# Inverse in tiles of 32 weight columns with its convolution taps moved, and the gate's input split during the PLE tiles

## The reference, cut to what matters

```python
qkv = silu(causal_conv(qkv, conv_buf, conv_w))          # four taps
a_mat = einsum("bnhid,bnhjd->bnhij", k_beta, k) * decay * strict
t_mat = triangular_solve(eye + a_mat, eye, lower=True, unit_diagonal=True)
...
e = rmsnorm(p_i @ w_proj, norm_w)                       # p_i has 256 columns
gate = sigmoid(h @ w_gate)                              # h has 2048 columns
h = h + e * gate
```

## Time and profile before

| | us |
| --- | --- |
| median of three runs | 2442.74 (2442.17 to 2444.59) |
| the profiled execution | 2443.26 |
| its span | 2441.5 |
| GDN loop, 15 passes | 971 |
| one pass of it | 63.54 |
| SSD loop and last body | 618 |
| first PLE step up to the second gate tile | 34 |
| PE busy | 2346.2 (96%) |
| POOL busy | 1762.6 (72%) |
| DVE busy | 1604.1 (66%) |
| ACT busy | 1260.5 (52%) |

### The profile page before, as it was taken

The page is one execution under the profiler, slowest core; times in us unless marked ns, Lnnn a source line. Parts: engine busy times, 40 slices in busy tenths (PEclk is TensorE's granted clock), DMA queues, the critical chain, the costliest instruction groups (busy, mean ns, idle before and its releaser), DMA issues.

```text
span 2441.5 us, 58796 instructions
## 1 busy us (share of the span) xinstructions
PE 2346.2 (96%) x21280; PEld 2201.1 (90%) x21280; DVE 1604.1 (66%) x3203; ACT 1260.5 (52%) x2201; POOL 1762.6 (72%) x2236
## 2 busy tenths in 40 slices
PE   5899999999999999999998989999999999999997
PEld 5799999999999999989998978989998999899897
DVE  7667666666666676661217466988898889712374
ACT  4555555555555555543335446555555555433443
POOL 5466566565555555558887968988898889789896
PEclk9999999999999999999999989999999999999998
DMA  5444444444444444436443445766576656554433
GB/s 200 149 156 148 155 155 148 151 142 148 144 155 147 148 143 143 146 114 222 155 164 134 163 152 204 239 202 202 189 240 212 198 193 229 189 182 155 155 136 123
DMA packets 126772, 410.84 MB, mean 168 GB/s; under 512 B 21344, under 2 KB 37984, under 8 KB 122112
## 3 DMA queue, kind: packets, MB, share of 16 engines
q1 hardware_dynamic: 80784, 294.49, 35.3%
q10 hardware_dynamic: 45936, 115.64, 14.0%
HBM read 363.47 MB, written 46.61 MB: 168 GB/s over the span
## 4 chain that ended last, share of the span: by engine, by line
PE 53%; POOL 32%; issue 10%; DVE 3%; ACT 1%; POOLq 0%; DMA 0%; DVEq 0%; ACTq 0%
POOL wl L335 32%; PE psj L358 14%; PE psj L359 12%; PE psj L360 12%; PE psA L393 2%; PE psC L393 2%; PE psE L393 2%; PE psD L504 1%; PE psA L569 1%; PE psC L519 1%; DVE xl L1398 1%; PE psA L382 1%; PE psE L535 0%; PE psE L387 0%; PE psC L387 0%
## 5 line engine op out<-in xcount | busy, mean ns | idle before, releaser
L335 POOL TENSOR_TENSOR wl<-ring,wh 128x256 fp32r<-128x256 f32 x2232 | 1762.4, 822 | 656.2 <-ACT wh L806 651.8
L358 PE MATMUL psj<-xh,wh 128*128 128x288 f32 x4400 | 1358.0, 309 | 37.2 <-DVE xl L1413 17.0
L359 PE MATMUL psj<-xl,wh 128*128 128x288 f32 x4400 | 1305.1, 297 | 0.0
L360 PE MATMUL psj<-xh,wl 128*128 128x288 f32 x4400 | 1300.3, 296 | 0.0
L358 PEld LDWEIGHTS psj<-xh,wh 128*128 128x128 f32 x4400 | 831.4, 189 | 90.9 <-issue 52.7
L806 ACT ACTIVATE wh<-ring 128x1024 fp32r<-128x1024 f32 x558 | 586.1, 1059 | 596.1 <-PE psj L360 556.9
L359 PEld LDWEIGHTS psj<-xl,wh 128*128 128x128 f32 x4400 | 834.2, 190 | 1.9
L360 PEld LDWEIGHTS psj<-xh,wl 128*128 128x128 f32 x4400 | 835.0, 190 | 0.0
L887 ACT ACTIVATE arena<-psj 128x256 f32<-128x256 f32 x112 | 42.8, 383 | 206.7 <-PE psj L360 200.5
L1768 DVE TENSOR_TENSOR h<-h,psj 128x288 f32 x32 | 14.5, 454 | 154.9 <-PE psj L360 154.9
L1839 DVE SCALAR_TENSOR_TENSOR arena<-arena 128x256 f32<-128x256 f32 x144 | 111.3, 799 | 3.4
(11 more groups left out here) (345 smaller groups left out, 2935.5 us busy)
## 6 DMA issues: line engine op xcount, KB each, us to landing
ring<-weights_d SPq DMA_DIRECT2D x558, 512.0 KB, 3.3
h<-gstate_d ACTq DMA_DIRECT2D x16, 1024.0 KB, 6.3
gst_s_d<-h ACTq DMA_DIRECT2D x16, 1024.0 KB, 3.9
h<-sstate_d ACTq DMA_DIRECT2D x32, 512.0 KB, 5.6
sst_s_d<-h ACTq DMA_DIRECT2D x32, 512.0 KB, 4.1
arena<-g_rows_d ACTq DMA_DIRECT2D x16, 864.0 KB, 6.0
arena<-s_rows_d ACTq DMA_DIRECT2D x8, 1152.0 KB, 8.7
h_spill_d<-h ACTq DMA_DIRECT2D x2, 2304.0 KB, 7.2
```

Source lines behind the costliest of these rows:

```text
L335: ins = pool.tensor_tensor(wl[:, s, n:n + 2], ring[:, s, n:n + 2], wh[:, s, n:n + 2].bitcast(F32), ALU.subtract)
L358: pe.matmul(out, w_h, xh[:, kt, :], start=(kt == 0), stop=False)
L359: pe.matmul(out, w_h, xl[:, kt, :], start=False, stop=False)
L360: mm = pe.matmul(out, w_l, xh[:, kt, :], start=False, stop=(kt == KT - 1))
```

## The change

Four parts. In `blocks` a call takes 32 weight columns instead of 64, so a group has twice the calls. The products read the same 32 columns of the right side as before. Of DVE's taps, the three prompt taps of v head 0 move from the inverse to the end of the pass before (`v_first`), between the norm and `Y`, with a wait for `took_act`. One tap of head 1 moves to the start of the body; the rest is spread anew, and the mask of level 4 comes behind the last sample taps. In the SSD loop two state products come one step later (46 and 56), and the sum one step later (71). In `ple` ACT and DVE split `h` during the projection, in slots 0 to 13 of `xh` and `xl`, while `dp` uses slots 14 and 15; the squares come later; and `e_sum` moves from step 4 to step 6.

```diff
-                for r in (0, 64):
-                    mm = pe.matmul(bank[r:r + 64, u * 32:(u + 1) * 32], lhsT[:, r:r + 64], rhs[:, in_block(r, lv), :],
+                for r in (0, 32, 64, 96):
+                    mm = pe.matmul(bank[r:r + 32, u * 32:(u + 1) * 32], lhsT[:, r:r + 32], rhs[:, in_block(r, lv), :],
...
-                    if e == 4 and late is not None:
+                    if e == 6 and late is not None:
...
-                at_smp, at_xt, at_states, at_sum = (33, 36, (45, 55), 70) if more else (41, 46, (54, 62), 72)
+                at_smp, at_xt, at_states, at_sum = (33, 36, (46, 56), 71) if more else (41, 46, (54, 62), 72)
...
+            def v_first():
+
+                do.link(v_tap(0, 0, 0))
+                do.link(v_tap(0, 1, 0))
+                v_tap(0, 2, 0)
+
             def gdn_body(m, full):
 
+                v_tap(1, 0, 0)
                 dve.wait_ge(S("g_tok"), m + 1)
...
                 if full:
                     gdn_qk_norm(m + 1)
+                    dve.wait_ge(took_act, m * 6 + 11)
+                    v_first()
...
+            def ple(tp, te, xp, xe, td, layer, hq):
...
                     dve.tensor_copy(eb[:, i, :], psj[(tp + i) % 2][:, 0:T]).then_inc(took_dve, 1)
-                    if i % 2 == 0 and i:
-                        dve.wait_ge(S("esq"), layer * KT + i)
-                        dve.tensor_tensor(eq[:, i - 2, :], eq[:, i - 2, :], eq[:, i - 1, :], ALU.add)
-                dve.wait_ge(S("esq"), layer * KT + KT)
-                do.link(dve.tensor_tensor(eq[:, KT - 2, :], eq[:, KT - 2, :], eq[:, KT - 1, :], ALU.add))
-                lower_x(lambda kt: h[:, kt, :], KT, xe)
+                    if i % 2:
+                        lower_h(i // 2)
+                for kt in range(KT // 2, KT):
+                    lower_h(kt)
+                for i in range(2, KT + 1, 2):
+                    dve.wait_ge(S("esq"), layer * KT + i)
+                    ins = dve.tensor_tensor(eq[:, i - 2, :], eq[:, i - 2, :], eq[:, i - 1, :], ALU.add)
+                do.link(ins)
```

More of the change, by code:

```diff
@@ L82 @@
 SMP_ACT = {n: i + 1 for i, n in enumerate(("asc", "kmc", "qs", "vnds"))}
-G_DVE_LINKS, S_DVE_LINKS = 19, 40
+G_DVE_LINKS, S_DVE_LINKS = 16, 40
 S_CONV = ((0, 2), (2, 4), (4, 5), (5, 6))
@@ L662, in ple @@
                         at = (2 * i + kt) % 8
-                        pe.matmul(out, wh[:, hc % 4, at, :], xh[:, kt, :], start=(kt == 0), stop=False)
-                        pe.matmul(out, wh[:, hc % 4, at, :], xl[:, kt, :], start=False, stop=False)
-                        mm = pe.matmul(out, wl[:, hc % 4, at, :], xh[:, kt, :], start=False, stop=(kt == PLE_K - 1))
+                        x = KT - PLE_K + kt
+                        pe.matmul(out, wh[:, hc % 4, at, :], xh[:, x, :], start=(kt == 0), stop=False)
+                        pe.matmul(out, wh[:, hc % 4, at, :], xl[:, x, :], start=False, stop=False)
+                        mm = pe.matmul(out, wl[:, hc % 4, at, :], xh[:, x, :], start=False, stop=(kt == PLE_K - 1))
                     if i % 4 != 3:
@@ L1125, in ple, with square_out, round_h @@
                 act.wait_ge(S("p_in"), 16 + es)
-                split_x(lambda kt: dp[:, kt, :], PLE_K, tp)
+                act.wait_ge(half_done, 2 * tp)
+                for kt in range(PLE_K):
+                    act.activation(xh[:, KT - PLE_K + kt, :], dp[:, kt, :], ACT.Copy).then_inc(xh_ready, 1)
                 ahead(0, 0, tp + 1)
[L1128 to L1132, removed]
+                def square_out(i):
                     act.wait_ge(took_dve, td + i + 1)
                     act.activation(eq[:, i, :], eb[:, i, :], ACT.Square).then_inc(S("esq"), 1)
+                def round_h(kt):
+                    act.activation(xh[:, kt, :], h[:, kt, :], ACT.Copy).then_inc(xh_ready, 1)
+                act.wait_ge(took_dve, td)
+                for kt in range(KT - PLE_K):
+                    round_h(kt)
+                    if kt in (5, 9, 13):
+                        upper(0, 0, 2 * te + (kt - 5) // 4)
+                for i in range(3):
+                    square_out(i)
+                upper(0, 0, 2 * te + 3)
+                for kt in range(KT - PLE_K, KT):
+                    round_h(kt)
+                for i in range(3, 10):
+                    square_out(i)
+                upper(0, 0, 2 * te + 4)
+                for i in range(10, KT):
+                    square_out(i)
+                upper(0, 0, 2 * te + 5)
                 def gate(i, k):
@@ L1147, in square @@
                         .then_inc(S("hsq"), 1)
-                act.wait_ge(took_dve, td)
-                split_x(lambda kt: h[:, kt, :], KT, te, second=True)
-                ahead(0, 0, te + 2)
                 act.wait_ge(S("ess"), hq // KT)
@@ L1537, in gdn_prepare, with v_tap @@
                 do.link(dve.tensor_tensor(u4(gAT[:, :, :]), u4(gDT[:, :, :]), beta, ALU.mult))
+            def v_tap(i, j, part):
+                a, b, at = ((0, SEQ, j), (SEQ, T, UC + DEC_B * j))[part]
+                out = gCR[:, 2 + i, a:b]
+                return dve.scalar_tensor_tensor(out, gU[:, 2 + i, at:at + b - a], gpc_tap[1][:, i, j:j + 1],
+                                                out, ALU.mult, ALU.add)
+            def v_first():
+                do.link(v_tap(0, 0, 0))
+                do.link(v_tap(0, 1, 0))
+                v_tap(0, 2, 0)
             def gdn_body(m, full):
+                v_tap(1, 0, 0)
                 dve.wait_ge(S("g_tok"), m + 1)
@@ L1561, in gdn_body @@
                 ins.then_inc(S("g_mk"), 1)
[L1563 to L1568, removed]
                 def parts(lv):
@@ L1604, in gdn_body @@
                 mask_p(0)
-                do.link(v_tap(0, 0, 0))
+                v_tap(1, 1, 0)
                 less_q(0)
@@ L1608, in gdn_body @@
                 mask_p(1)
-                do.link(v_tap(1, 0, 0))
+                v_tap(1, 2, 0)
                 less_q(1)
-                v_tap(1, 0, 1)
-                do.link(v_tap(0, 1, 1))
+                do.link(v_tap(1, 0, 1))
                 mask_p(2)
-                do.link(v_tap(0, 1, 0))
+                v_tap(0, 1, 1)
                 less_q(2)
-                do.link(v_tap(1, 1, 0))
+                do.link(v_tap(1, 1, 1))
                 mask_p(3)
@@ L1744, in _ @@
             dve.wait_ge(took_act, 6)
+            do.link(v_tap(0, 0, 0))
+            do.link(v_tap(0, 1, 0))
+            do.link(v_tap(0, 2, 0))
             with dve.Fori(0, GH - 1) as m:
@@ L1772, in ple, with lower_h @@
             def ple(tp, te, xp, xe, td, layer, hq):
-                lower_x(lambda kt: dp[:, kt, :], PLE_K, xp)
+                def lower_h(kt):
+                    dve.wait_ge(xh_ready, xe + kt + 1)
+                    dve.tensor_tensor(xl[:, kt, :], h[:, kt, :], xh[:, kt, :].bitcast(F32), ALU.subtract) \
+                        .then_inc(xl_ready, 1)
+                for kt in range(PLE_K):
+                    dve.wait_ge(xh_ready, xp + kt + 1)
+                    x = KT - PLE_K + kt
+                    dve.tensor_tensor(xl[:, x, :], dp[:, kt, :], xh[:, x, :].bitcast(F32), ALU.subtract) \
+                        .then_inc(xl_ready, 1)
                 for i in range(KT):
```

5 lines of the change are left out of this document (1 added, 4 removed).

## The result

| | us | against before |
| --- | --- | --- |
| before | 2442.65 (2442.17 to 2444.59) | |
| changed | 2534.14 (2523.82 to 2543.79) | 1.0372 (1.0353 to 1.0391) |

The changed kernel is 91 us slower, far above the range. Its profiled execution has a span of 2522.0 us, 80.5 more than before. A pass of the GDN loop, from one start of DVE's body to the next, went from 63.5 us to 69.0 us in the mean (66.6 to 71.2), so the loop alone gives +81.5 us. The first pass starts 2.5 us later, the last GDN body gives 2.7 back, and from the first PLE step to the end the execution is 0.7 shorter, the SSD loop's gain less the loss of the two PLE steps.

What follows compares the result with a forecast made beforehand. PE, busy 96% of the span, was taken as the bound; 2443.26 + 0 (GDN loop) - 4.5 (SSD loop) + 0.5 (PLE stages) = 2439.3, so 2439 us, range 2420 to 2461.

Steps and rivals of the forecast that it cites:

- the tiles of 32 columns: Groups of the GDN loop's inverse: 0.25 us instead of 0.46, saving PE 3.15 us a pass, 47 us in 15 passes.
- The rivals on the slower side: Two alternatives: a longer DVE-ACT-PE cycle with falling clock (chance 0.30), and 32-column tiles no faster (chance 0.04).
- That the tiles are no faster: Rival in the inverse: records start 0.029 us apart at best, 2549 us; at the old 0.46 us, 2484; chance 0.04.
- that the clock falls: Rival in the GDN loop: new PE waits lower the clock, +12 us, 2451 to 2463; chance 0.30 with a longer cycle.
- the wait at step 5: PE at line 440 in each GDN pass, waiting some 2 us for DVE's line 1546.
- The ring: DVE, ACT and PE waiting on each other each GDN pass: 63.53 us beside 63.54, so the loop changes by 0.
- arcs: Five consecutive stretches of a GDN pass over PE, ACT and DVE: 10.54, 8.3, 6.83, 15.1 and 22.76 us.
- arc 4: From the first mask to psC of level 5 in the inverse: 15.1 us (14.7 to 15.8), before 18.02.
- arc 2: From ACT's count 11 to DVE's line 1544 of the next pass: 8.3 us (7.0 to 9.4), 2.9 later than before.
- The first pass: First GDN pass: linked taps cost 2.5 us more before and in it, its inverse gives 2.5 back, net 0.
- SSD: SSD loop: PE's waits at line 753 for DVE's line 1957 go, a gain of 4.5 us (2.5 to 5.5).
- The gate's input: Both PLE stages: projection waits removed, but a new 4 us wait at line 382; +0.5 us (-8 to +7).

## Why the prediction was wrong

**The step that failed is the first, the tiles of 32 columns.** Its time was right: 0.26 us a group where I wrote 0.25, 3.15 us a pass of PE's work. What it left out is that twice the calls are also twice the instructions: 480 in a loop of 1485. I had no term for it and no rival, although the page has a line for the instruction queue, and my first group of rows counts PE's instructions. In its place the runs showed a fetch of ten blocks in each pass: 5.6 us a pass in stalls and 2.4 in clock, 120 us, less 47 that the tiles save. The rivals on the slower side name other causes. That the tiles are no faster, 2549 us, comes near in time, and for the wrong reason; that the clock falls was half right, but it falls behind the fetches, not behind the wait at step 5.

**The ring** was right in kind, as the kernels without fetches show. By arcs: 10.54 as forecast; 7.39 for 8.3; 6.91 for 6.83; arc 4 was 17.62 with no fast level, 17.26 with levels 0 and 1 and 15.9 with levels 2 to 4 (63.51 less the other arcs), where I took 15.1 for all five; 22.74 for 22.76. Two errors of the opposite sign: arc 2 is 0.9 shorter, and in levels 0 and 1 DVE's taps hold the level, so the tiles give 0.36 instead of 1.26 there. (The bounds were not added up rightly: the arcs' own give 61.8 and 65.3 for a pass, not 61.6 and 65.1, and arc 2's least values give 6.6, not 7.0. The forecast doesn't hang on it.) With all five levels fast the ring would give 63.2 us or so; no loop of that size fits, so that isn't measured. In the trace of the changed kernel the taps themselves hardly show: PE's waits at line 440 come in only two passes, since the fetches make PE late first.

**The first pass** started 2.5 us later, as forecast. **SSD**: -4.5 forecast, -3.6 measured. **The gate's input**: forecast +0.5 for both, measured +6, a second term with the wrong size. The stage in the changed kernel:

```profile
1388.05 0.29 PE L666 MATMUL psj<-xh,wl 128*128 128x288 f32 x1
1388.89 0.40 PE L358 MATMUL psj<-xh,wh 128*128 128x288 f32 x1 [0.55 <-DVE Y L1813]
...
1405.99 0.85 PE L382 MATMUL psB<-Y,cst 128*128 128x288 f32 x1 [4.83 <-DVE Y L1824]
```

```profile
1388.75 7.77 DVE L1800 TENSOR_TENSOR xl<-h,xh 128x288 fp32r<-128x288 f32 x9
1396.44 6.81 DVE L1820 TENSOR_TENSOR Y<-Y 128x288 f32<-128x288 f32 x8
```

```profile
1404.12:1414.36 10.24, 7.42 (x27) 6.79 (x28) 8.08 (x10) 4.39 (x6) 3.76 (x5) 0.50 0.15 50
```

The idle stretch ahead of the gate fell from 3.44 to 0.55 us, as I wrote, and PE waits 4.83 us at line 382, where I wrote 4. Two terms were too small. DVE's 17 operations took 14.6 us, not 12.8, so the sum comes 17.9 us behind the last matmul, not 17.3: 1.3 later than before, less the 0.9 that the projection gained. And I had put the half clock behind that wait in the shadow of the sigmoid. It lasts until 1414.36, 8.4 us behind the wait, and so covers most of the third tile; the fourth tile starts 30.2 us behind the last matmul of the projection, where it started 26.3 behind it before. So 2.7 us are lost behind the sum, in each of the two steps, where I took 0.5 for both. Together that is 0.4 + 2.7 = 3.1 us a step, the 6 us measured.

## What to carry to other kernels

When an edit adds instructions to a loop, count them as code too: find how many the loop has, where it starts, and look at the packets of the instruction queue before and after. More packets than the program has blocks mean that a loop is being fetched again, and the profile then shows it as waits for issue, at fixed places, with no engine's name or with that of one that had long been done. A faster instruction sequence that needs more instructions is best used only in the places where PE is the bound, and in so many that the loop still fits.

## What the runs showed of the hardware

In these 20 kernels PE kept a loop that touches 7 blocks of 256 instructions (35 to 38 packets in all); one that touches 8 or 9 was fetched with 9 or 10 packets of 16 KB in each pass (162 to 179 in all), and 72 idle instructions ahead of the loop changed the time by 100 us in one pair and 198 us in another. The block count has one number in it that was fitted, the 51 instructions ahead of the kernel's own. The stalls vary from pass to pass: passes of the changed kernel range from 66.6 to 71.2 us, and its executions over 20 us, where those of before stay within 3 in the same comparison; what sets their length wasn't tested. Behind two stalls of 1.4 and 1.9 us the granted clock was 0.50; behind one of 1.3 us it stayed 1.00. It also fell for 31 us behind 3 us of small transposes with no idle time at all, in five of 15 passes.
